# A fourth group of products computed during the first condition products, and an earlier first inverse root, in a one-core decoder layer on Trainium2

## What is computed

```python
ada = jnp.dot(jax.nn.silu(c), p["w_ada"]) + p["b_ada"]
sh1, sc1, gt1, sh2, sc2, gt2 = jnp.split(ada[:, None, :], 6, axis=-1)
h = _rmsnorm(x, p["g_norm1"]) * (1.0 + sc1) + sh1
(qkv_raw, z, a_raw, b_raw, dq, dk, dv, iq, ik, iw, gate_gdn, gate_dsa) = _split_cols(jnp.dot(h, p["w_in"]))
...
o_gdn = _rmsnorm(o_gdn.astype(x.dtype), p["g_gdn_norm"]) * jax.nn.silu(z.reshape(B, T, GDN_HEADS, GDN_DV))
...
mix = (jax.nn.sigmoid(gate_gdn) * jnp.dot(o_gdn, p["w_gdn_out"])
       + jax.nn.sigmoid(gate_dsa) * jnp.dot(o_dsa, p["w_dsa_out"]))
```

## Time and profile before

| | us |
|---|---|
| median of 3 runs | 1914.02 (1913.17 to 1914.82) |
| profiled execution, its own time | 1918.98 |
| its span | 1917.2 |
| PE busy in it | 1860.1 (97%) |
| POOL, ACT, DVE busy | 1187.7, 806.3, 653.1 |

### The profile page before, as it was taken

How to read it: one execution, slowest core, us unless ns; L and a number is a source line. 1 busy time by engine, 2 the same in 40 slices (tenths; PEclk the granted TensorE clock), 3 DMA queues, 4 the chain that set the end, 5 groups by cost and what they waited for, 6 DMA issues and landing times.

```text
span 1917.2 us, 41582 instructions
## 1 busy us (share of the span) xinstructions
PE 1860.1 (97%) x16712; PEld 1750.3 (91%) x16712; DVE 653.1 (34%) x1783; ACT 806.3 (42%) x1353; POOL 1187.7 (62%) x508
## 2 busy tenths in 40 slices
PE   6999999999999999999999999999999999999997
PEld 2689999999888878888999899999999999999996
DVE  3227764444414242322442433220132231123333
ACT  3344445665323222323434655543344443344442
POOL 0266666665444344435877677777777777777773
PEclk9999999999999999999999999999999999999998
DMA  9966654444787878789764455555555455555552
GB/s 390 408 248 217 197 154 142 143 154 132 228 298 246 296 257 291 241 294 296 226 236 159 155 166 165 166 166 167 168 165 164 164 165 166 165 168 166 167 184 83
DMA packets 145614, 391.24 MB, mean 204 GB/s; under 512 B 27778, under 2 KB 36450, under 8 KB 144834
## 3 DMA queue, kind: packets, MB, share of 16 engines
q1 hardware_dynamic: 125488, 374.56, 58.2%
q10 hardware_dynamic: 19986, 14.70, 2.5%
HBM read 379.70 MB, written 8.88 MB: 203 GB/s over the span
## 4 chain that ended last, share of the span: by engine, by line
PE 89%; DMA 4%; DVE 3%; issue 1%; ACT 1%; DVEq 1%; POOL 1%; SPq 0%; ACTq 0%; POOLq 0%; PEldq 0%
PE bank L2407 26%; PE bank L2408 26%; PE bank L2412 26%; PE bank L2367 3%; DMA raw_c<-in_stream 2%; DMA raw_a<-in_stream 1%; PE bank L2889 1%; PE bank L2356 1%; PE bank L2341 1%; POOL rest_a L835 0%; PE bank L2758 0%; PE bank L2774 0%; PE bank L2626 0%; DVE x L2331 0%; ACT hi_a L895 0%
## 5 line engine op out<-in xcount | busy, mean ns | idle before, releaser
L835 POOL TENSOR_TENSOR rest_a<-raw_a,hi_a 128x1024 fp32r<-128x1024 f32 x168 | 402.8, 2399 | 239.3 <-ACT hi_a L895 239.2
L2407 PE MATMUL bank<-h_hi,hi_a 128*128 128x288 f32 x1720 | 474.8, 302 | 3.0 <-ACT hi_a L895 2.7
L2408 PE MATMUL bank<-h_lo,hi_a 128*128 128x288 f32 x1720 | 465.5, 296 | 0.0
L2407 PEld LDWEIGHTS bank<-h_hi,hi_a 128*128 128x128 f32 x1720 | 325.2, 189 | 21.3 <-issue 15.9
L2408 PEld LDWEIGHTS bank<-h_lo,hi_a 128*128 128x128 f32 x1720 | 326.1, 190 | 0.2
L895 ACT ACTIVATE hi_a<-raw_a 128x1024 fp32r<-128x1024 f32 x168 | 177.8, 1059 | 282.5 <-PE bank L2412 210.7
L835 POOL TENSOR_TENSOR rest_b<-raw_b,hi_a 128x1024 fp32r<-128x1024 f32 x74 | 178.4, 2411 | 106.8 <-ACT hi_a L895 106.7
L2412 PE MATMUL bank<-h_hi,rest_a 128*128 128x288 f32 x1488 | 226.5, 294 | 1.3 <-POOL rest_a L835 1.3
L2412 PEld LDWEIGHTS bank<-h_hi,rest_a 128*128 128x128 f32 x1488 | 207.0, 188 | 1.7 <-POOL rest_a L835 1.6
L2407 PE MATMUL bank<-h_hi,hi_b 128*128 128x288 f32 x648 | 177.2, 300 | 0.0
L2408 PE MATMUL bank<-h_lo,hi_b 128*128 128x288 f32 x648 | 175.2, 296 | 0.0
(11 more groups left out here) (531 smaller groups left out, 3783.2 us busy)
## 6 DMA issues: line engine op xcount, KB each, us to landing
raw_a<-in_stream SPq DMA_DIRECT2D x364, 512.0 KB, 3.7
raw_b<-in_stream SPq DMA_DIRECT2D x179, 512.0 KB, 3.6
raw_c<-in_stream SPq DMA_DIRECT2D x94, 512.0 KB, 3.4
raw_m<-in_stream SPq DMA_DIRECT2D x27, 512.0 KB, 6.1
raw_e<-in_stream SPq DMA_DIRECT2D x12, 512.0 KB, 9.1
st<-in_state ACTq DMA_DIRECT2D x8, 512.0 KB, 6.3
st<-in_state SPq DMA_DIRECT2D x8, 512.0 KB, 6.3
out_state_s<-st ACTq DMA_DIRECT2D x8, 512.0 KB, 7.0
```

The costliest lines, as they stand in the source:

```text
L835: nc.gpsimd.tensor_tensor(rest_in(name, r), raw_of(name, r), w_hi[q].bitcast(f32), ALU.subtract).then_inc(lo_ready, 1)
L2407: MM(banks[c][:, 0:N], w_, hi_of(k), start=(first and k == 0), stop=False)
L2408: ins = MM(banks[c][:, 0:N], w_, lo_of(k), start=False, stop=False)
```

## The change

A fourth group is added to the early ones: the first of the four z groups. EARLY then has 16 products, and the stage "in" has 24 groups (two z groups after the dsa ones, and the last). A load order with RAW_E = 4 buffers and LEAD = 5 is used. Groups 0 and 1 are held in banks 0/1 and 2/3 through all quarters, while groups 2 and 3 take turns in banks 6/7: after each quarter DVE copies it out or adds it to what it has (`evict`), and the next quarter that uses these banks waits for that. The first silu of z is taken from there (`early_z`). The stage "in" starts in banks 2/3 instead of 0/1.

The first inverse root moves: all four squares are added on DVE after group 0 and summed on PE in group 2, the first half of x is squared when it has arrived, and a logarithm without use is put ahead of the squares (`early_ln`). ACT's and DVE's order of the remaining steps is written anew. Semaphores are merged, which changes no order. The core of the diff, with the merges, the bank names and the slot arithmetic left out:

```diff
-N_DSA, N_Z, N_QKV, N_IN = 1, 1 + DSA_T // CT, (DSA_T + Z_T) // CT, 1 + (DSA_T + Z_T + QKV_T) // CT
+N_DSA, N_Z, N_QKV, N_IN = 1, 1 + DSA_T // CT, (DSA_T + Z_T) // CT - 1, (DSA_T + Z_T + QKV_T) // CT
...
-N_EARLY = 3
-EARLY = [(e % N_EARLY, e // N_EARLY) for e in range(N_EARLY * (KT // KS))]
-EARLY_AT = {(7, 0): (0,), (8, 0): (1,), (9, 0): (2,), (10, 0): (3,), (11, 0): (4,), (12, 0): (5,), (14, 0): (6,), (15, 4): (7, 8)}
+N_GATE, N_HELD, N_EARLY = 3, 2, 4
+QUARTER = ((2, 0, 3, 1), (2, 0, 3, 1), (2, 0, 3, 1), (1, 2, 0, 3))
+EARLY = [(g, s_) for s_, order in enumerate(QUARTER) for g in order]
+TURNS_OF = [e for e, (g, _) in enumerate(EARLY) if g >= N_HELD]
+EARLY_AT = {(5, 2): (0,), (6, 1): (1,), (7, 0): (2,), (7, 3): (3,), (9, 0): (4,), (9, 3): (5,), (10, 2): (6,), (11, 1): (7,),
+            (13, 0): (8,), (13, 3): (9,), (14, 2): (10,), (15, 4): (11,)}
 E_IN = N_EARLY * (KT // KS - 1)
-LEAD, RAW_E = 4, 3
+LEAD, RAW_E = 5, 4
+
+
+def early_bank(e):
+
+    g, s_ = EARLY[e]
+    return 2 * g if g < N_HELD else 6
...
-    return BASE["small"] + j + (KT // KS if n >= N_QKV else 0)
+    if n < N_QKV and n >= N_Z:
+        return BASE["z"] + (n - N_Z + 1) * (KT // KS) + s
+    if n >= N_QKV:
+        return BASE["qkv"] + (n - N_QKV) * (KT // KS) + s
+    return BASE["small"] + j
...
         assert sq_.at <= qkv_at
...
-                act.wait_ge(x_in, 32)
+                act.wait_ge(x_back[q // 2], 16)
...
+                e = EARLY.index((g, KT // KS - 1))
+                act.wait_ge(early_done, e + 1)
                 for c in range(CT):
-                    last = A_(park[CT * g + c], bank[E_BANK[g] + c][:, 0:N], ACT.Copy)
+                    last = A_(park[CT * g + c], bank[early_bank(e) + c][:, 0:N], ACT.Copy)
...
 
+            def early_z():
+
+                act.wait_ge(evicted, len(TURNS_OF))
+                for c in range(CT):
...
+            act.wait_ge(const_in, 48)
+            early_ln()
             for q in range(4):
                 square_quad(q)
-            act.wait_ge(const_in, 48)
             rms(0)
             round_pair(0)
             round_pair(1)
             round_samples(0)
-            hi("early", 0)
+            for e in range(3):
+                hi("early", e)
             round_pair(2)
-            hi("early", 1)
-            hi("early", 2)
+            hi("early", 3)
+            hi("early", 4)
+            hi("early", 5)
             round_pair(3)
             round_samples(1)
-            hi("early", 3)
+            hi("early", 6)
+            hi("early", 7)
             round_pair(4)
-            hi("early", 4)
-            hi("early", 5)
+            hi("early", 8)
+            hi("early", 9)
+            hi("early", 10)
             round_pair(5)
             round_samples(2)
-            hi("early", 6)
+            hi("early", 11)
+            hi("early", 12)
             round_pair(6)
-            for e in (7, 8, 9):
-                hi("early", e)
+            hi("early", 13)
             round_pair(7)
             round_samples(3)
-            hi("early", 10)
-            hi("early", 11)
-            for g in range(N_EARLY):
+            hi("early", 14)
+            hi("early", 15)
+            keep_early(1)
+            for g in range(2):
                 hi("in", g)
-                keep_early(g)
+            keep_early(0)
+            hi("in", 2)
...
                     z_tiles(n - 1)
+                    if n - 1 == N_Z:
+                        early_z()
...
+            def evict(e):
+
+                g, s_ = EARLY[e]
+                dve.wait_ge(early_done, e + 1)
+                for c in range(CT):
+                    to, of = park[CT * g + c], bank[early_bank(e) + c][:, 0:N]
+                    last = CP(to, of) if s_ == 0 else T_(to, to, of, ALU.add)
+                last.then_inc(evicted, 1)
...
             for n in range(2 * KT // CT):
                 if n >= 1:
                     cond_copy(n - 1)
                     if n == 1:
                         dve.wait_ge(const_in, 48)
+                    if n == 7:
+                        evict(2)
+                    if n == 9:
+                        evict(4)
+                    if n == 13:
+                        evict(8)
                     cond_bias(n - 1)
-                if n in (2, 3):
-                    add_squares(2 * n - 4)
-                    add_squares(2 * n - 3)
-                if n in (4, 5):
-                    if n == 4:
-                        dve.wait_ge(rs_ready, 1)
-                    scale_x(2 * n - 8)
-                    scale_x(2 * n - 7)
-                if n == 5 or n in (8, 12):
-                    samples(n // 4 - 1)
-                if n == 5:
+                if n == 1:
+                    for q in range(4):
+                        add_squares(q)
+                if n == 3:
+                    dve.wait_ge(rs_ready, 1)
+                    scale_x(0)
+                    scale_x(1)
+                if n == 4:
+                    samples(0)
                     lo_pair(0)
-                if n == 6:
                     lo_pair(1)
                     lo_samples(0)
-                if n >= 7 and n % 2:
-                    lo_pair((n - 3) // 2)
-                if n in (9, 13):
-                    lo_samples((n - 5) // 4)
+                    scale_x(2)
+                if n == 5:
+                    scale_x(3)
+                    evict(0)
+                if n >= 6 and n % 2 == 0:
+                    if n % 4 == 0:
+                        samples(n // 4 - 1)
+                    lo_pair(n // 2 - 1)
+                    if n % 4 == 0:
+                        lo_samples(n // 4 - 1)
+                if n == 10:
+                    evict(6)
+                if n == 14:
+                    evict(10)
             cond_copy(2 * KT // CT - 1)
             cond_bias(2 * KT // CT - 1)
             samples(3)
             lo_pair(KT // CT - 1)
             lo_samples(3)
+            evict(13)
+            evict(15)
             dve.drain()
...
-                if n == N_QKV - 1:
+                if n == N_QKV:
...
+                held = g < N_HELD
+                if e == 0:
                     pe.wait_ge(xr_ready, 4)
+                elif not held:
+                    pe.wait_ge(evicted, TURNS_OF.index(e))
                 pe.wait_ge(hs_lo, s_ + 1)
                 pe.wait_ge(h_hi_ready, (s_ + 1) * KS)
-                slot("early", e, lambda k: h_hi[:, s_ * KS + k, :], lambda k: h_lo[:, s_ * KS + k, :], (bank[E_BANK[g]], bank[E_BANK[g] + 1]),
-                     s_ == 0, s_ == KT // KS - 1, tiles=HB + s_ * KS)
+                slot("early", e, lambda k: h_hi[:, s_ * KS + k, :], lambda k: h_lo[:, s_ * KS + k, :], (bank[early_bank(e)], bank[early_bank(e) + 1]),
+                     s_ == 0 or not held, s_ == KT // KS - 1 or not held, tiles=HB + s_ * KS)
...
-                    if s_ == 3 and n in (2, 3):
-                        first_sum(2 * n - 4)
-                        first_sum(2 * n - 3)
-            early(E_IN - 2)
+                    if (n, s_) == (2, 1):
+                        for q in range(4):
+                            first_sum(q)
+            early(E_IN - 1)
             turn(2 * KT // CT - 1)
-            for e in range(E_IN - 1, len(EARLY)):
+            for e in range(E_IN, len(EARLY)):
                 early(e)
...
+                pe.wait_ge(evicted, len(TURNS_OF))
```

More of the change, by code:

```diff
@@ L120, in in_slot @@
         return BASE["qkv"] - KT // KS + s
-    return BASE["small"] + j + (KT // KS if n >= N_QKV else 0)
+    if n < N_QKV and n >= N_Z:
[3 more added lines that the diff above has]
+    return BASE["small"] + j
 N_LATE = KT // KS * 2
-NA, ND = 4 * KT // CT * (KT // KS) - N_LATE, (KT // CT) * (2 * (KT // KS) + H // KS) - len(EARLY)
+NA, ND = 4 * KT // CT * (KT // KS) - N_LATE, (KT // CT) * (2 * (KT // KS) + H // KS) - N_GATE * (KT // KS)
 FILL = ("DAADAADAADAAD" + "DAADAADAADAA") * (NA // 16) + "DAADAADAADAAD"
-D_GROUPS = [g for m in range(KT // CT) for g in (("gd", m, KT // KS), ("ds", m, H // KS)) if m >= N_EARLY or g[0] == "ds"] \
+D_GROUPS = [g for m in range(KT // CT) for g in (("gd", m, KT // KS), ("ds", m, H // KS)) if m >= N_GATE or g[0] == "ds"] \
     + [("gg", m, KT // KS) for m in range(KT // CT)]
@@ L190, in early_slot @@
     m, s = EARLY[e]
-    return BASE["out"] + 12 * m + 4 + s
+    return BASE["out"] + 12 * m + 4 + s if m < N_GATE else BASE["z"] + s
 def go_slot(j):
@@ L471, in decoder_step @@
         assert gq.at >= tp.at
-        park_a = Place(gq.at).take("park_a", [P, CT * N_EARLY - 1, N])
-        park = [park_a[:, t, :] for t in range(CT * N_EARLY - 1)] + [qkv[:, QKV_T - 4, :]]
-        assert gq.at + 4 * (CT * N_EARLY - 1) * N <= nc.sbuf_usable_end
+        park_a = Place(gq.at).take("park_a", [P, 5, N])
+        park = [park_a[:, t, :] for t in range(5)] + [qkv[:, t, :] for t in (QKV_T - 4, QKV_T - 5, QKV_T - 1)]
+        assert len(park) == CT * N_EARLY and jp.at <= qkv_at + 4 * (QKV_T - 5) * N
```

(20 more changed lines are left out.)

31 lines of the change are left out of this document (14 added, 17 removed).

## The result

The change makes the kernel slower. Its median is 1926.7 us (1920.6 to 1931.0, six runs) beside 1914.4 us of the kernel before on the same chip, a ratio of 1.0051 with a 95% interval of 1.0037 to 1.0065. So the loss is some 10 to 13 us, and the two intervals together reach from 7 to 16. The prediction, 1921.7, had the sign and the three waits. Its size was too small by the median, since 1926.7 lies above the top of its range (1924.5). By the ratio the first comparison can't tell: 1921.7 is 1.0040 of 1914.0, inside the first interval, while the second interval begins just above the top of the range, 1.0055. The profiled execution after took 1931.0 us, the longest of the six, with a span of 1929.1, so 11.9 more than before.

What follows compares the result with a forecast made beforehand. Loads pace the early slots at 1.28 us each, then PE limits. "In" 3.0 us past break-even plus 4.7 for low clock gives 7.7 us slower: 1914.0 + 7.7 = 1921.7 us, range 1914.0 to 1924.5.

Steps and rivals of the forecast that it cites:

- What bounds the kernel, and the break-even: Loads pace the early slots, then PE limits; stage "in", one group shorter (12.7 us), breaks even starting at 136.1.
- Step 1, the start: Early products from product 0 on: start at 43.5, a 2.3 us stall before product 4, PE at (13,0) at 93.0.
- Step 2, the first ACT block: Before product 8: ACT rounds weight 10, load landing at 93.3, ahead of pair 5; PE idles 4.5 us.
- Step 3, the second ACT block: At turn 14: rounding 12 delays pair 6, DVE's copy stands behind its subtraction; PE idles 4.0 us, until 117.0.
- Step 4, the end: After turn 15, product 12 waits the full 4.16 us; "in" at 139.1, 3.0 us slower than break-even at full clock.
- Step 5, the clock: Behind the three long PE stalls: low clock costs 3 x 1.57 = 4.7 us.
- The sum: Whole kernel: 3.0 plus 4.7 gives 7.7 us slower, added to the 1914.0 median: 1921.7.
- The stalls leave the clock alone: Rival on PE's clock after the stalls: only +3.0 us, 1917.0; chance 0.18.
- ACT's order does not hold up DVE: Rival at pair 6: load 12 lands before its factor is ready; 5.1 us faster, 1908.9; chance 0.12.
- The earlier root does nothing: Rival at the start: product 0 no earlier, product 8 at 98.9; +9.0 us, 1923.0; chance 0.08.
- The index stall: PE stall before the index products, 3.54 us; rival that it grows or goes, 3.54 + 1.57 either way, chance 0.05.
- What costs nothing: Other evictions, early_z's two extra silus and SP's later start of "in" loads were taken to add no time.

Runs made afterwards that it cites:

- e9: e8 with DVE's lo_pair, lo_samples and samples in the rounds of the kernel before, behind the next copy and bias: ratio 0.9982 to the kernel before.
- e11: e10 with ACT's rounding 12 ahead of pair 6 again: ratio 0.9977 to the kernel before.
- e4: Changed kernel with rounding 12 behind pair 6, rounding 10 behind pair 5 and its samples, product 11 behind turn 15: ratio 0.9998 to the kernel before.
- e6: Changed kernel with the inverse root later (sums behind slot (3,3), x scaled in round 4): ratio 1.0097 to the kernel before.
- e1: Changed kernel with ACT's rounding 12 moved behind pair 6: ratio 1.0031 to the kernel before.
- e2: Changed kernel with DVE's lo_pair(6) behind the copy and bias of group 14, ACT's order kept: ratio 1.0025 to the kernel before.
- e3: Changed kernel with early product 11 behind the last turn, not ahead of it: ratio 1.0036 to the kernel before.
- e5: Changed kernel with ACT's rounding 10 moved behind pair 5 and its samples: ratio 1.0040 to the kernel before.
- e12: Changed kernel run once more, nothing edited, as a reference and second trace: ratio 1.0070 to the kernel before.
- e8: Changed kernel with e4's ACT edits, products 4 to 9 at later slots, product 10 ahead of the last turn and 11 behind: ratio 1.0013 to the kernel before.
- e10: e9 with ACT's rounding 13 behind the last pair and its samples: ratio 0.9970 to the kernel before.

## Why the prediction was right in sign and too small

- **What bounds the kernel, and the break-even.** This held, to 2 or 3 us. "In" 13.5 late gave 11.9 us in the span, and the kernels with "in" ahead of 136.1 (e9 to e11) are the ones that are faster; e4, 2.3 behind it, is level.
- **Step 1, the start.** Product 0 started at 44.27 (43.5 predicted), the stall before product 4 was 2.29 (2.3), and PE was at product 8's place at 100.81 - 5.49 = 95.3 (93.0). Of the missing 2.3 us 0.8 are the start and 1.3 the slow start of product 0: it took 6.0 us to the next slot, where I had 4.74 from the kernel before.
- **Step 2, the first ACT block.** This was right in mechanism: there is a stall of 5.49 (4.5). Rounding 10's load came at 96.5 and not at 93.3. The term that failed is "It is load number 64 of the stream ... 38.26 + 43 x 1.28". That takes the loads for continuous, but they are released by PE's progress, and PE was late. From 50 to 100 us the loads ran at 401, 377, 370, 390 and 401 GB/s, where the kernel before had 406 to 409: 1.0 MB less, or 2.5 of the 3.2 us. For the same reason "the date of the root has hardly any say" was wrong: I priced a late root at 1.3 us, and in e6 "in" comes 5.4 later, 1.5 of it by the clock.
- **Step 3, the second ACT block.** This was right in mechanism, with a wait of 4.93 (4.0), and it is shown by e1 and e2, each of which removes it alone. Its date was 6.4 us late (117.0 predicted, 123.45): 3.2 carried from step 2, 1.7 for product 8's low clock, and 1.7 for the load behind (15,3), which landed 6.4 us after (13,3) was used up (111.9) and not 4.7, less 0.3 on the way from there to the turn.
- **Step 4, the end.** This was right. The chain took 135.23 - 131.07 = 4.16, as predicted, with nothing in it, since product 11 stands ahead of the turn. e3 shows that the stall is that order's.
- **Step 5, the clock.** I predicted 3 x 1.57 = 4.7. The first products behind the three stalls cost 1.7 (105.93 - 100.81 = 5.12 for 3.38), 2.3 (7.62 from turn 14 to the last turn for the 5.3 of steps 3 and 4) and 1.6 (14.3 for four products of 12.7): 5.7. What I had left out is that the clock's loss comes before the next step's load is released, and moves it as well. I gave a shorter stall no such cost. Before product 4 that was right after and in e5, but in e6 the same 2.3 us cost 1.5 there, and in e4 and e5 they cost 1.5 before product 8. What tells these cases apart is open: neither the length nor the place does. The rule of the Trainium skill (TensorE: Matmul & The Clock Gate, section Why this matters for your kernels) held at all three long stalls.
- **The sum.** 143.8 (139.1 and 4.7) was predicted for "in"; 149.6 came, 5.8 later: 3.2 from step 2, 1.5 more from step 3 (the load, less the 0.3) and 1.0 more for the clock. The mechanism was right, and three of its terms were too small.
- **Rivals.** "The stalls leave the clock alone" fell. "ACT's order does not hold up DVE" fell: load 12 came 4.6 us after the factor. "The earlier root does nothing" fell, as e6 shows. The index stall stayed, 3.69 (3.54). "What costs nothing" held: evictions alone made no wait (e2).

Undoing parts one by one moved "in" by 8.9, 7.5, 5.7 and 4.3 us, but these are not terms to be added. e1 and e2 remove the same wait, and the edits' own gains are 7.2 for either of them, 3.1 for e3 and 3.4 for e5, so 13.7 for the three waits. e4 has all three and gains 11.5 from the slots ahead of product 8 on; 1.8 of the difference is its longer last chain (5.93 instead of 4.16). The same kernel twice (e12) differs by 0.7 over that stretch.

## What to carry to other kernels

When a rounding of weights is put ahead of a step of the main chain on an in-order engine, ask when its load lands, and give that date a margin: a load stream that waits for buffers is no clock, and every delay of PE comes back as a later load. A moved product uncovers the chain that it covered; look for what the next wait on the same chain is (here the copy behind the subtractions), before counting the gain. In these runs the extra group paid (0.2 to 0.3% in e9 to e11) once each turn had a product, or five slots and the next turn, between itself and its first user, and once copies that PE waits for stood ahead of work that hangs on a load. Three slots, as before product 8, were not enough: that left 2.3 us.

## What the runs showed of the hardware

A VectorE instruction on two SBUF operands waited for GpSimd's running subtraction. The factor ended at 120.30 + 2.07 = 122.37 in e8, where GpSimd's instruction ended at 119.94 + 2.39 = 122.33; alone it takes 0.18. The bias ahead of it, which reads a PSUM bank and one SBUF operand, ran in 0.18 at 120.03, inside the same GpSimd instruction. The Trainium skill says this (SBUF — State Buffer, section "SBUF: two separate sides"): the port pair that VectorE shares with GpSimd is locked for a whole instruction by the one that starts first, and a VectorE operation with two SBUF inputs needs it when GpSimd's reads SBUF. The traces agree, in both directions of that distinction. It is no single case: in e9 the factor of pair 5 ended at 94.31, GpSimd's instruction at 94.28, and in e10 at 94.52 and 94.48, and this is what held up turn 12 there. In e11, where no GpSimd instruction runs beside it, the same factor took 0.18 (at 92.53). On a chain of 4.16 us this is up to 1.9 us, and which instruction is hit changes from one version to the next.
